# A hybrid decoder block rewritten as a new program: folded weight products, token-major softmax, interleaved halves

## The reference, cut to what matters

```python
h = rms_norm(x, norm_mix)
b_a, c_a, u_a, u_p, q_x, g_a, g_p, g_x = split(h @ w_in)        # eight blocks of 1024 columns
y_a = (b_a * causal_dwconv3(c_a * u_a)) @ w_conv_out
pooled = trailing_mean(u_p, window 2/4/8/16 per group of 256 channels) - u_p
y_p = (pooled @ w_pool, a 256x256 map per group) * pool_scale
k, v = split(rms_norm(mem, norm_mem) @ w_kv)                     # 256 memory tokens
o = softmax(q_x @ k.T / 16) @ v                                  # 4 heads of 256
y_x = o @ w_xattn_out
merged = sigmoid(g_a) * y_a + sigmoid(g_p) * y_p + sigmoid(g_x) * y_x
x = x + merged @ w_out
h = rms_norm(x, norm_ffn)
x = x + (silu(h @ w_gate) * (h @ w_up)) @ w_down                 # 2816 inner columns
out = rms_norm(x, norm_final)
```

## Time and profile before

| | us |
|---|---|
| median of 3 runs | 1209.54 (1209.42 to 1209.95) |
| the profiled execution, its own time | 1209.65 |
| span of its slowest core (core 4) | 1208.1 |
| TensorE (PE) busy | 1151.4 |
| VectorE (DVE) busy | 512.1 |
| ScalarE (ACT) busy | 298.4 |

### The profile page before, as it was taken

One profiled execution on the slowest core, in us unless ns is written; L12 is line 12 of the kernel. 1 busy time (PEld: TensorE's weight loads), 2 busy tenths in 40 slices (PEclk: granted clock), 3 DMA queues, 4 the chain that ended last, 5 costly groups with the idle time before them and its releaser, 6 DMA issues.

```text
span 1208.1 us, 14601 instructions; the slowest of 8 cores (1206.3 to 1208.1 us)
## 1 busy us (share of the span) xinstructions
PE 1151.4 (95%) x5615; PEld 535.1 (44%) x5720; DVE 512.1 (42%) x504; ACT 298.4 (25%) x412; POOL 77.5 (6%) x150
## 2 busy tenths in 40 slices
PE   2999999999999999999999999999999989999997
PEld 1454444444444444444444444444444444444443
DVE  4117888633336122212460778863333621221135
ACT  5432322211115211011463222221111431101122
POOL 2110000000000100100000000000000010000000
PEclk9999999999999999999999999999999999999998
DMA  9998433245543980099654333325553398009103
GB/s 236 193 166 144 70 53 54 43 79 87 88 91 119 167 138 1 12 153 176 164 177 79 67 58 68 50 38 88 87 88 79 113 151 137 1 1 152 31 18 122
DMA packets 29140, 115.95 MB, mean 96 GB/s; under 512 B 3200, under 2 KB 3328, under 8 KB 28560
## 3 DMA queue, kind: packets, MB, share of 16 engines
q0 software_dynamic: 21024, 85.50, 43.0%
q1 hardware_dynamic: 8048, 29.51, 7.3%
HBM read 192.10 MB, written 8.39 MB: 166 GB/s over the span
## 4 chain that ended last, share of the span: by engine, by line
PE 80%; DVE 10%; DMA 4%; issue 3%; ACT 2%; DVEq 0%; SPq 0%; ACTq 0%
PE ps L182 79%; DMA arena<-x 3%; DVE rden L558 2%; DVE tmp L477 1%; DVE tmp L474 1%; DVE tmp L508 1%; DVE tmp L512 1%; DVE tmp L467 1%; DVE arena L519 1%; DVE tmp L504 1%; PE ps L277 1%; ACT junk L262 1%; DVE arena L561 1%; DMA tmp<-x 1%; ACT tmp L472 0%
## 5 line engine op out<-in xcount | busy, mean ns | idle before, releaser
L182 PE MATMUL ps<-arena,ring 128*128 128x512 bf16 (+1 forms) x4074 | 869.0, 369 | 19.5 <-ACT arena L284 3.8
L182 PEld LDWEIGHTS ps<-arena,ring 128*128 128x128 bf16 x4160 | 392.4, 98 | 487.7 <-issue 24.1
L717 DVE TENSOR_TENSOR arena<-ps,tmp 128x1024 bf16<-128x1024 f32 x44 | 53.9, 1225 | 254.5 <-PE ps L182 239.8
L182 PE MATMUL ps<-arena 128*128 128x512 bf16 x689 | 152.5, 379 | 0.8
L714 ACT ACTIVATE tmp<-ps 128x1024 f32<-128x1024 f32 x44 | 45.0, 1023 | 319.4 <-PE ps L182 319.4
L182 PEld LDWEIGHTS ps<-arena 128*128 128x128 bf16 x704 | 68.7, 98 | 81.9
L735 DVE TENSOR_TENSOR arena<-ps,arena 128x1024 f32<-128x1024 f32 x32 | 39.2, 1224 | 80.5 <-PE ps L182 80.5
L175 POOL DMA_DIRECT2D ring<-w_in x64 | 33.9, 530 | 470.2 <-PE ps L182 418.6
L262 ACT ACTIVATE junk<-arena 128x1024 bf16<-128x1024 f32 x40 | 42.1, 1052 | 63.8 <-DVE stat L266 27.4
L182 PE MATMUL ps<-ring,arena 128*128 128x512 bf16 x256 | 56.9, 379 | 0.3 <-DVE stat L266 0.3
L558 DVE RECIPROCAL rden<-ps 128x512 f32<-128x512 f32 x16 | 53.6, 3347 | 0.0
(11 more groups left out here) (72 smaller groups left out, 582.5 us busy)
## 6 DMA issues: line engine op xcount, KB each, us to landing
ring<-w_in POOLq DMA_DIRECT2D x64, 512.0 KB, 7.3
ring<-w_gate_up POOLq DMA_DIRECT2D x44, 512.0 KB, 25.3
arena<-w_down POOLq DMA_DIRECT2D x4, 2816.0 KB, 21.7
arena<-x SPq DMA_DIRECT2D x4, 2048.0 KB, 18.8
out<-tmp SPq DMA_DIRECT2D x16, 512.0 KB, 2.9
arena<-x SPq DMA_DIRECT2D x8, 512.0 KB, 13.8
ring<-w_kv POOLq DMA_DIRECT2D x8, 512.0 KB, 27.9
ring<-w_conv_out POOLq DMA_DIRECT2D x8, 512.0 KB, 6.2
```

The source lines that it names most:

```text
L182: ins = e.matmul(o, l, r, start=s0, stop=s1)
L717: dve(lambda e, u=u, sg=sg, c=c: e.tensor_tensor(out=actT[:, c, :], in0=PU[u][:, 0:TM], in1=sg[:, 0:TM], op=ALU.mult), reads=[("PU", u), ( ...
```

## The change

It is a new program for the same function, with the same division over the cores, the same planner and the same ring of 12 slots.

- Folded products. `a_fold` makes `A = w_q @ k.T / 16` (1024 channels x 4 heads x 256 memory tokens) once; `fold_g` makes, a group of 256 channels at a time, `w_p @ w_pool` and `v @ w_xattn_out`. All three are written to HBM scratch tensors as bf16 and loaded again in the second half. The query projection, the `P @ V` products, the denominators and the `w_pool` matmuls are gone. Host code packs two more, transposed copies of parts of `w_in`.
- Token-major softmax with maximum. `score` makes the scores of one tile of 128 tokens with 16 matmuls of 512 columns; DVE takes the negated maximum of each head, ACT does four `exp` with bias and sum, DVE a reciprocal and four scalings to bf16, and `score_t` transposes the tile on PE. 16 tiles in all.
- The history is 20 tokens, and a unit with history has three blocks of 348 columns (3 x 348 = 20 + 1024) in three banks. All 8 banks of PSUM are handed out in rotation by `banks`.
- Pooling moved behind the folded projection, into `merge_chunk`.
- Halves interleaved: the norm of the second half is done inside the convolutions of the first, `w_out` and the second norm of the first half inside the convolutions of the second (`o_step`), `w_out` of the second half inside the gate and up chunks of the first (`o1`), and its norm inside the down stage of the first. `x` after the mixer goes through a scratch tensor in HBM. The 22 inner chunks are done in one pass, `w_down` is loaded once and stays (`wdT`).
- The opening: the convolution's weights are asked for at once, without a wait for `x`, and the first units (convolution, C) are begun by blocks while the last tiles are still being normalized.

```diff
-HALO = 16
+HALO = 20
+B3 = TH // 3
+    def score(H, i):
+        b = banks(2)
+        ...
+                mms.append((bank(b + hp), H.rhs(kc, i * P, P), A_sc[:, kc, hp * 512:(hp + 1) * 512],
+                            kc == 0, kc == KC - 1))
+        pe(mms, H.keys(i * P, P) + kA(A_M, 8), kB(b, 2))
+        ...
+        dve(lambda e: e.tensor_reduce(out=sm[:, c:c + 4], in_=bank(b, 2).rearrange("p (h m) -> p h m", h=4),
+                                      axis=AX.X, op=ALU.max, negate=True), kB(b, 2), [("sm", c)])
+        for h in range(4):
+            act(lambda e, h=h: e.activation(out=ex[:, h * 256:(h + 1) * 256], in_=PS[:, b * 512 + h * 256:b * 512 + (h + 1) * 256],
+                                            func=AF.Exp, bias=sm[:, c + h:c + h + 1], scale=1.0,
+                                            accum_out=sm[:, c + 4 + h:c + 5 + h]),
+                kB(b, 2) + [("sm", c)], ek + [("sm", c + 4 + h)])
+        dve(lambda e: e.reciprocal(out=sm[:, c + 8:c + 12], in_=sm[:, c + 4:c + 8]),
+        ...
+        for h in range(4):
+            dve(lambda e, h=h: e.tensor_scalar(out=pr[:, h * 256:(h + 1) * 256], in0=ex[:, h * 256:(h + 1) * 256],
+                                               scalar1=sm[:, c + 8 + h:c + 9 + h], scalar2=None, op0=ALU.mult),
+                ek + [("sm", c + 8)], [hbi.key()])
+        return (hbi, i)
+    def s_step(H, i):
+        s_pend.append(score(H, i))
+        if len(s_pend) > 1:
+            score_t(s_pend.pop(0))
+    ...
+    conv_units(0, H0, 2, cs[1])
+    b_batch(0)
+    conv_units(0, H0, 3, cs[1], [b_trans, b_trans, b_trans])
+    b_trans()
+    cs[2] = conv_slots(2)
+    ...
+    a_fold(ws["q"])
+    b_batch(1)
+    kv_proj(ws["v"], vT, "vT")
+    ...
+    for j in range(4, 8):
+        ...
+        conv_units(0, H0, j, cs[j // 2], [f0, None, f2])
+    folded = fold_g(0, sP0, sX0)
+    score_t(s_pend.pop(0))
+    merge(0, H0, folded)
+    ...
+    order = [[0, 1, 2], [3, 4, 5], [6, 7], []]
+    for j in range(4):
+        conv_units(1, H1, j, cs[j // 2], [(lambda i=i: o_step(i)) for i in order[j]])
+    ...
+    for j in range(4, 8):
+        k = 2 * (j - 4)
+        conv_units(1, H1, j, cs[j // 2], [(lambda k=k: s_step(H1, k)), None, (lambda k=k: s_step(H1, k + 1))])
+    score_t(s_pend.pop(0))
+    merge(1, H1, None)
+    ...
+    ffn(0)
+    ffn(1)
```

More of the change, by code:

```diff
@@ new lines, in banks, with kB, bank, __init__ @@
+    def banks(n):
+        p = st["pb"]
+        while True:
+            if p + n > 8:
+                p = 0
+            if any((p + i) in held for i in range(n)):
+                p += 1
+                continue
+            st["pb"] = (p + n) % 8
+            return p
+    def kB(b, n):
+        return [("B", i) for i in range(b, b + n)]
+    def bank(b, n=1):
+        return PS[:, b * 512:(b + n) * 512]
+    gen = {}
+    class Ref:
+        def __init__(self, kind, i):
+            self.kind, self.i = kind, i
+            self.g = gen[(kind, i)] = gen.get((kind, i), 0) + 1
+        def key(self):
+            assert gen[(self.kind, self.i)] == self.g, (self.kind, self.i)
+            return (self.kind, self.i)
@@ L183, in fn @@
             return ins
[L184 to L219, removed]
@@ L236, in proj_end @@
[L236 to L242, removed]
-    def act(fn, reads, writes):
-        plan.op("act", fn, reads=reads, writes=writes)
-    def dve(fn, reads, writes):
-        plan.op("dve", fn, reads=reads, writes=writes)
-    def gps(fn, reads, writes):
-        plan.op(POOL_ADD_ENGINE, fn, reads=reads, writes=writes)
@@ L254, in new_stat, with next_hb, hbt, cols @@
+    def next_hb():
+        b = Ref("hb", st["hb"] % 4)
+        st["hb"] += 1
+        return b
+    def hbt(b):
+        return hb[b.key()[1]]
+    def cols(n):
         c = st["stat"] % 32
[L255 to L269 removed]
@@ L747, in build_program @@
[L747 to L764 removed]
+        sGa, sCo, sGp, sPC, sGx, sVO = S
@@ new lines, in build_program, with a_step @@
+    pend = []
+    def a_step(i):
+        pend.append((a_tile(i), i))
+        if len(pend) > 2:
+            a_trans(*pend.pop(0))
+    for i in range(6):
+        a_step(i)
+    uc = [proj(cs[0][0], jj, H0, halo=True) for jj in range(2)]
+    for u in uc:
+        held.update(range(u.b, u.b + 3))
+        u.block(0)
+    a_step(6)
+    a_step(7)
+    a_step(8)
+    for u in uc:
+        u.block(1)
+    while pend:
+        a_trans(*pend.pop(0))
+    for u in uc:
+        u.block(2)
+    held.clear()
@@ new lines, in build_program, with conv_units @@
+    for mt in range(2):
+        transpose(mem_b[mt], memT[:, :, mt * P:(mt + 1) * P], kA(40, 2))
+    def conv_units(hf, H, j, slots, between=()):
+        sC, sU, sB = slots
+        jj = j % 2
+        tb = 0 if jj == 0 else 3
+        bt = list(between) + [None] * 3
+        halo = hf == 0
+        u = proj(sC, jj, H, halo=halo).run()
+        conv_a(j, u, tb)
+        if bt[0]:
+            bt[0]()
+        u = proj(sU, jj, H, halo=halo).run()
+        conv_b(hf, j, u, tb)
+        if bt[1]:
+            bt[1]()
+        u = proj(sB, jj, H).run()
+        conv_c(j, u)
+        if bt[2]:
+            bt[2]()
```

1081 lines of the change are left out of this document (543 added, 538 removed).

## The result

The new kernel took 1233.2 us in the median of the runs shown with it, the old one 1209.5: ratio 1.022 (95% interval 1.015 to 1.029). It is slower, by some 2%, where 1177 had been predicted. On a second chip, in five rounds, 1235.5 against 1210.4, ratio 1.021 (1.0195 to 1.022).

A forecast was written before the change was run, and what follows sets the result against it. PE work was taken to bound the kernel; PE work -27.1, opening -3, middle waits -1 and tail -1.4 sum to -32.5 us, from 1209.65 to 1177, range 1168 to 1188 (60%).

The forecast's parts named there:

- PE work, -27.1: Matmuls and transposes on PE, both halves: removed work against added work, priced per matmul, saves 27.1 us.
- 24.6 us of waits in the middle: Old kernel between opening and tail: PE idle 24.6 us, from 56.7 less 8.4 and 23.7.
- The opening, -3 with bounds -7 to +5: Before the first projections: early units gain 6 us, x comes 3 later; -3 us, bounds -7 to +5.
- The weights in the first 100 us, +6: Loads until the values are projected: PE waiting for weights costs 6 us, bounds 0 and 15; called the main risk.
- The softmax chain: Score tiles through DVE and ACT to probabilities: 5.6 us, covered inside the loop; waits of 2 and 5 us at its ends.
- Rival 4: Whole kernel: PE with fewer gaps is granted less clock; 11 us for each 1%, 1233 at 5%; chance 1%.
- my own list of new waits: Middle of the new kernel: mem transposes 2, score ends 7, last norm 3, weights 6, others; 24 against 24.6, so -1.
- The tail, -1.4: After the last matmul: each tile's norm follows its add, so DVE ends earlier, -1.4 us.
- Rival 3: Score stages: a maximum or exp as costly as the reciprocal makes the chain the bound, 1225 us; chance 5%.

The follow-up runs named there:

- the filled one: New kernel with matmuls that nobody reads added at nine places where PE waits: 1224.8 us, beside 1235.5 for the unchanged new kernel on the same chip.
- the last kernel: New kernel with its orders repaired twice, and the maximum left out as well (exp with a bias of zero): 1177.6 us, ratio 0.973 to the old kernel.
- the keys gated: New kernel with the keys' weight load, and all loads after it, waiting for the eighth tile of x: 1223.0 and 1225.0 us.
- the fill's first run: New kernel with unread matmuls added in nine waits, on another chip than its repeat: 1229.4 us, ratio 1.015 to the old kernel.
- the kernel with the repairs: New kernel with opening loads behind x, all nine transposes before the first units, and transposes of scores, mem, o_step and last norm reordered: 1206.2 us, ratio 0.996.

## Why the prediction was wrong, by its steps

- *PE work, -27.1*: held. In the new trace 24 matmuls of 348 columns take 196.30 - 192.75 = 3.55 us, 64 of 256 take 7.0; both are the prices used. At the full clock the real work goes from 1151.4 + 6 in the old kernel (holes counted in, next point) to 1130 in the filled one, 27 less. That the last kernel takes 1177.6, the number predicted, is in part luck: it has no maximum, and its PE is busy 1136.5 us and idle 40.4, where the forecast had 1124 and 51.
- *The baseline of it*: "24.6 us of waits in the middle" was too much. The old profile has 5615 matmuls for 5720 weight loads: 105 records are missing, and each leaves a hole of some 55 ns that looks idle (two spacings of 217 ns less the 379 of one matmul), 5.8 us in all. By the prices the old PE work was 1159 us, the new 1132; the old waits in the middle were some 19, which is also what the profile's list of them adds up to.
- *The opening, -3 with bounds -7 to +5*: failed, by 21 us, and outside its bounds (PE is idle 41.9 us before the first U, where 23.7 - 3 = 20.7 had been forecast). The step said "three weight slots now share the DMA engines with x from the start". The trace has twelve, a full ring, and `w_pool` ahead of the first that waits for PE: POOL runs its own list, and what stands later in the program is not later in time. For three slots the +3 was right: with the keys gated, `x` is there at 30.0 us instead of 27.3, though the sum given for it (3.1 MB at 0.3 MB per us) makes 10 us and not 4. The gate that the old kernel had (`after=kA(0, 8)`) was read and not counted as something that the change removes. The old kernel without it shows its price, 20 us.
- *The weights in the first 100 us, +6*: failed the other way. PE never waited for a slot up to there. I had seen rightly that the engines are full (until about 68 us) and charged the wrong transfer: not the weights were late but `x`, behind which everything stands. (The terms given up to the values add to 92 us, not 95.)
- *The softmax chain, "nothing waits inside the loop", 7 at its ends*: the operations were right (maximum 1.22 for 1.2, scalings 1.74 for 1.5 a tile), `exp` was not: 474 ns each with its bias, not 382, so 2.5 us for four with their sums and not 2.3. The cover was counted from the end of the score tile, but in DVE's list the maximum stands behind the convolution's two sums and its last product, which end 1.6 us after the scores. So there are waits of 2.0 and 2.3 us for probabilities inside the two loops, and 10.1 at the ends (2.9 and 7.2) for 7.
- *The clock*: the step is missing. The forecast took the granted clock as fixed, since the old trace has it at 1.00 all along, and as a rival only a limit from dense work (1%). The fall came from the other side, behind waits. The old kernel never waits more than 1.3 us after its opening, so its clock column could not show this. Its opening shows it in the durations: eight transposes there take 1.01 us, as behind the wait up to 563.67 where the column has 0.50, and 0.61 us later on the earlier trace rows. The column reads 1.00 in the opening all the same, in both kernels, until its first change; in the new kernel 16 matmuls of 348 columns take 4.26 us at 34.81 with the column at 1.00, and 2.52 us at 57.02. In the new one (1 - 0.980) x 1231.6 = 24.6 us of full clock are missing, 3.6 in the old; PE's busy time is 16 us above its prices. The filled kernel puts 10.7 us on it in time. Rival 4 had 1233 for a clock that falls by 5%; that is the number measured, but by luck, since the mean fell by some 1.5%, behind waits, and did a third of the damage. The Trainium skill has the rule ("TensorE: Matmul & The Clock Gate", section "HAM oscillation — how this bites in real kernels": idle gaps of a few us drop the clock, and what follows runs cold), and this trace agrees; I weighed the page's other rule and left this one out, though my own list of new waits had entries of 5 and 7 us.
- *The tail, -1.4*: from the last matmul to the end it is 7.6 us and not 8.4: -0.8.

In sum against the predicted span of 1175.6, by idle and busy PE: opening 21.2; PE's busy time above its prices 16.0, which I put down to the clock; waits in the middle 34.2 for 23.6, so 10.6; the busy time that the old trace lacks 7.6 (1159 - 1151.4); tail 0.6: 56.0. Rival 3 gave nearly the right number (1225) for a wrong reason: the maximum costs what an ordinary operation costs. (DVE would have been full from a maximum of 5.05 us by the terms given, not 4.8.) The rule that the prediction quoted for it from the Trainium skill ("VectorE: DVE Perf Modes", section "The perf-mode tier table"), estimated there at 1.2 us, agrees with 1219 ns for 1024 columns.

## What to carry to other kernels

Ask of a queue what it can issue before its first true wait, not what stands near it in the program; a dependency that holds weights back behind the data which everything needs was worth 20 us here. A wait on PE can cost a stretch at half clock besides itself (here after two in three of the waits of 2.0 to 3.1 us and after nearly all longer ones), so a change that trades many short waits for a few long ones can lose more than the work it saves. Where a long chain (score, maximum, exp, scale, transpose) ends a stage, put units that don't need it between it and its user.

## What the runs showed that I had not expected

On the chip of the fill's first run a third clock appeared, for some 5 us at a time: on core 0 of the kernel with the repairs the stretch below has 0.88 over 5 us, with PE busy throughout and no wait ahead of it; microsecond by microsecond the column is 0.81 from 356 to 361.

```profile
354.00:359.00 5.00, 5.00 (x22) 2.17 (x21) 4.51 (x6) 1.04 (x2) 0.00 (x0) 0.88 1.03 167
```

The old kernel took 1210.8 there, 1.3 us more than on the first chip. The rule of the Trainium skill that the prediction called contradicted ("TensorE: Matmul & The Clock Gate", section "Seeing it yourself": 13/16 of the clock, 0.81, for a die with three or more cores in dense matmuls) thus has something to it. In this execution it came for a few short stretches, where the page has it held for as long as the load lasts; whether it was this limit, and what it cost, was not measured.
